# Hybrid decoder layer on one core: projection and sampled stage in one block, forget-attention queries projected last

## The reference, cut to what matters

```
z = h @ w_in                                  # 1056 tokens, 1024 -> 2848 columns
q_n, k_c, v_c, k_s, v_s, k_w, v_w, g, q_f, k_f, v_f, f = split(z)
logf = log_sigmoid(f + b_forget)
kc, vc = compress(k_c, cmp_pe[0], cmp_w1[0], cmp_w2[0]), compress(v_c, ...)   # gelu(flat @ w1) @ w2
o_n, o_f = attend_block(...)                  # compressed, selected, window branches; forgetting attention
x = x + rms_norm(concat(rms_norm(o_n), rms_norm(o_f)) @ w_o)
y = x + rms_norm((silu(hf @ w_gate) * (hf @ w_up)) @ w_down)
```

## Time and profile before

| | us |
|---|---|
| median of 3 runs | 1807.78 (1803.63 to 1809.15) |
| the profiled execution, its own time | 1804.37 |
| its span, first to last instruction | 1802.7 |
| PE busy | 1719.0, 95% of the span |
| DVE / ACT / POOL busy | 1008.4 / 724.4 / 304.3 |
| projection's last product ends, us from the start of the span | 315.5 |
| first matmul with w1 | 338.69 |

### The profile page before, as it was taken

One profiled execution on the slowest core, in us unless ns is written; L12 is line 12 of the kernel. 1 busy time (PEld: TensorE's weight loads), 2 busy tenths in 40 slices (PEclk: granted clock), 3 DMA queues, 4 the chain that ended last, 5 costly groups with the idle time before them and its releaser, 6 DMA issues.

```text
span 1802.7 us, 35393 instructions
## 1 busy us (share of the span) xinstructions
PE 1719.0 (95%) x13557; PEld 1573.7 (87%) x13557; DVE 1008.4 (56%) x1892; ACT 724.4 (40%) x1439; POOL 304.3 (17%) x629
## 2 busy tenths in 40 slices
PE   8999999799887999999999999999999999999998
PEld 6999999676665888788876899999999999999998
DVE  4533342223364666666665577766566664566565
ACT  5101010222233777777875541333333332344343
POOL 3000015320503435354430000000000000000000
PEclk9999999899998999999999999999999999999998
DMA  5547976645999212030202242232222325131112
GB/s 140 193 132 185 228 221 117 191 144 175 310 341 285 77 28 81 14 94 1 95 1 77 83 144 67 73 104 75 72 72 76 103 72 222 60 123 48 44 47 103
DMA packets 146081, 212.63 MB, mean 118 GB/s; under 512 B 23993, under 2 KB 102248, under 8 KB 145858
## 3 DMA queue, kind: packets, MB, share of 16 engines
q1 hardware_dynamic: 114114, 143.36, 24.9%
q0 software_dynamic: 16480, 52.41, 9.5%
q10 hardware_dynamic: 15328, 14.72, 3.4%
HBM read 163.11 MB, written 51.49 MB: 119 GB/s over the span
## 4 chain that ended last, share of the span: by engine, by line
PE 69%; DVE 6%; ACT 3%; issue 2%; DMA 1%; POOL 0%; DVEq 0%; SPq 0%; ACTq 0%
PE psum L195 14%; PE psum L197 13%; PE psum L196 13%; PE psum L2112 5%; PE psum L2085 5%; PE psum L1177 4%; PE psum L2076 3%; PE psum L2077 2%; PE psum L1198 2%; DMA fox_ring<-in_cache_fox_kv 1%; PE psum L1240 1%; PE psum L2120 1%; PE psum L1159 1%; PE psum L2105 1%; ACT h_parts L3182 1%
## 5 line engine op out<-in xcount | busy, mean ns | idle before, releaser
L195 PE MATMUL psum<-h_parts,down_hi 128*128 128x352 f32 x528 | 171.7, 325 | 5.9 <-DVE h_parts L3383 4.3
L195 PE MATMUL psum<-x_hi,w_hi 128*128 128x352 f32 x528 | 170.7, 323 | 1.3 <-issue 1.3
L196 PE MATMUL psum<-h_parts,down_hi 128*128 128x352 f32 x528 | 170.5, 323 | 0.0
L197 PE MATMUL psum<-h_parts,down_lo 128*128 128x352 f32 x528 | 170.5, 323 | 0.0
L196 PE MATMUL psum<-x_lo,w_hi 128*128 128x352 f32 x528 | 170.4, 323 | 0.0
L197 PE MATMUL psum<-x_hi,w_lo 128*128 128x352 f32 x528 | 170.3, 323 | 0.0
L195 PE MATMUL psum<-hf_hi,op_hi 128*128 128x264 f32 x576 | 163.5, 284 | 0.6 <-DVE silu L3364 0.6
L197 PE MATMUL psum<-hf_hi,op_lo 128*128 128x264 f32 x576 | 163.5, 284 | 0.0
L196 PE MATMUL psum<-hf_lo,op_hi 128*128 128x264 f32 x576 | 163.3, 284 | 0.0
L2165 ACT ACTIVATE probs<-psum,neg_max 128x640 f32<-128x640 f32 (+7 forms) x192 | 139.8, 728 | 18.3 <-DVE neg_max L2323 9.0
L2085 PE MATMUL psum<-ident,probs 128*128 128x128 f32 x848 | 129.1, 277 | 4.0 <-ACT probs L2165 2.4
(11 more groups left out here) (455 smaller groups left out, 4254.3 us busy)
## 6 DMA issues: line engine op xcount, KB each, us to landing
fox_ring<-in_cache_fox_kv SPq DMA_DIRECT2D x128, 256.0 KB, 6.1
zT<-z_stage SPq DMA_DIRECT2D x22, 528.0 KB, 4.4
w_ring<-in_w_in POOLq DMA_DIRECT2D x22, 512.0 KB, 5.5
down_ring<-in_w_ffn_down SPq DMA_DIRECT2D x44, 256.0 KB, 2.7
raw<-in_w_ffn_gate SPq DMA_DIRECT2D x9, 1024.0 KB, 7.8
raw<-in_w_ffn_up SPq DMA_DIRECT2D x9, 1024.0 KB, 5.4
h_dram<-stage POOLq DMA_DIRECT2D x8, 1056.0 KB, 6.0
nsa_page<-in_cache_nsa_kv POOLq DMA_DIRECT2D x64, 128.0 KB, 6.2
```

What stands on the lines that cost most here:

```text
L195: nc.tensor.matmul(dst, w_hi, x_hi, start=start, stop=False, skip_group_check=onto)
L196: nc.tensor.matmul(dst, w_hi, x_lo, start=False, stop=False, skip_group_check=onto)
L197: return nc.tensor.matmul(dst, w_lo, x_hi, start=False, stop=stop, skip_group_check=onto)
```

## The change

The two blocks become one: `build_a` and `build_b` write into the same block, no barrier stands between them. A function `projected(eng)` waits until all stores of `zT` and `nat` have landed; SP waits for it at the end of the projection as before, and now POOL, ACT and DVE wait for it too ahead of their first work of the sampled stage (POOL also for the last `take` and the key parts). PE has no such wait: its first job in each bank waits for `z_copied` of the last tile in that bank (and for the turns' copies in banks 6 and 7). The plan's order becomes q_n, nsa_kv, win_kv, fox_kv, q_f. `w1` is issued in the q_n group; the pages of sequences 0 to 3 are issued one sequence after each pair of fox_kv; the last 16 forget rows go four at a time after each pair of fox_kv, not in a seam. `load_sampled` waits for the tiles ahead of q_f, loads the fox slices of `k_new`, and no longer loads `q_fox`, whose 8 loads now stand on POOL's queue behind `load_nsa(0)`. POOL reads its 32 page numbers ahead of the waits.

```diff
-             dict(name="win_kv", col=1024, pairs=1, turn=True), dict(name="q_f", col=1304, pairs=2, turn=False),
-             dict(name="fox_kv", col=1816, pairs=4, turn=True)]
+             dict(name="win_kv", col=1024, pairs=1, turn=True), dict(name="fox_kv", col=1816, pairs=4, turn=True),
+             dict(name="q_f", col=1304, pairs=2, turn=False)]
...
-        build_a(nc, a, o, c, env)
         middle = root.enter_context(ExitStack())
         env["block"] = middle.enter_context(nc.Block())
...
+        build_a(nc, a, o, c, env)
         build_b(nc, a, o, c, env)
...
+def projected(eng, env):
+
+    for s in range(2):
+        eng.wait_ge(env["zt_stored"][s], 16 + 16 * (NZ // 2))
+        eng.wait_ge(env["nat_stored"][s], NAT_STORED[s])
...
-        block = ctx.enter_context(nc.Block())
+        block = env["block"]
...
-                loop(sp, l["pairs"], pair)
+                if l["name"] == "fox_kv":
+                    for i in range(l["pairs"]):
+                        pair(i)
+                        load_lf(1, range(PAGES // 2 + i * PAGES // 8, PAGES // 2 + (i + 1) * PAGES // 8))
+                else:
+                    loop(sp, l["pairs"], pair)
...
-                        pool.dma_start(q_fox[e * DH:(e + 1) * DH, :, p * 40 + e * TS:p * 40 + (e + 1) * TS],
-                                       zT[TILE["q_f"] + p, e * DH:(e + 1) * DH, T:N].rearrange("d (s t) -> d s t", t=TS)).then_inc(new_loaded, 16)
+                    pool.dma_start(k_new[:, 2:6, :], zT[TILE["fox_kv"]:TILE["fox_kv"] + 4, :, T:N].rearrange("n p t -> p n t")).then_inc(new_loaded, 16)
...
-                if l["name"] == "q_f":
-                    act.wait_ge(gf_stored, 64)
+                if l["name"] == "q_n":
...
+                if l["name"] == "fox_kv":
+                    act.wait_ge(gf_stored, 64)
                     act.wait_ge(pages_loaded, 16)
-                    for b in range(4):
-                        load_sequence(act, a, pages, chunks, b, chunk_loaded[b // 2])
...
                     pair(i, [s for s in range(2) if l["n0"] + 2 * i + s in KEY_TILES])
+                    if l["name"] == "fox_kv":
+                        load_sequence(act, a, pages, chunks, i, chunk_loaded[i // 2])
...
-            pool.memset(chunksT[:, :, :, 4, :], 0.0).then_inc(cleared, 1)
-            pool.dma_start(k_new[:, 2:6, :], zT[TILE["fox_kv"]:TILE["fox_kv"] + 4, :, T:N].rearrange("n p t -> p n t")).then_inc(new_loaded, 16)
             pool.wait_ge(pages_loaded, 16)
             read_four(0)
+            pool.wait_ge(z_copied, NZ + 2)
+            projected(pool, env)
+            pool.wait_ge(env["key_stored"], 64 * len(KEY_TILES))
+            pool.memset(chunksT[:, :, :, 4, :], 0.0).then_inc(cleared, 1)
             load_nsa(0)
+            with nc.allow_non_contiguous_dma(reason="four tokens of a head"):
+                for h in range(H):
+                    p, e = h // 2, h % 2
+                    pool.dma_start(q_fox[e * DH:(e + 1) * DH, :, p * 40 + e * TS:p * 40 + (e + 1) * TS],
...
+                else:
+                    pe.wait_ge(z_copied, NZ + 1 if B.bank[job] < 3 else NZ + 2)
+                    if B.bank[job] >= 6:
+                        pe.wait_ge(turn_copied, 2 + 3 * NTURN)
...
+            projected(act, env)
             for st in range(2):
...
+            projected(dve, env)
             for st in range(2):
```

More of the change, by code:

```diff
@@ L171, in program @@
         env = dict(locals())
-        build_a(nc, a, o, c, env)
         middle = root.enter_context(ExitStack())
         env["block"] = middle.enter_context(nc.Block())
+        env["z_copied"], env["turn_copied"], env["key_stored"] = sem("z_copied"), sem("turn_copied"), sem("key_stored")
+        env["zt_stored"], env["nat_stored"] = [sem(f"zt_stored{s}") for s in range(2)], [sem(f"nat_stored{s}") for s in range(2)]
+        build_a(nc, a, o, c, env)
         build_b(nc, a, o, c, env)
@@ L289, in build_a @@
         key_high, key_low = env["key_high"], env["key_low"]
-        key_high_set, key_low_set, key_stored = sem("key_high_set"), sem("key_low_set"), sem("key_stored")
+        key_high_set, key_low_set, key_stored = sem("key_high_set"), sem("key_low_set"), env["key_stored"]
         key_parts = env["key_parts"]
@@ L306, in build_a @@
         z_done = sem("z_done")
-        z_copied = sem("z_copied")
-        zt_stored = [sem(f"zt_stored{s}") for s in range(2)]
+        z_copied, turn_copied, zt_stored, nat_stored = (env[k] for k in ("z_copied", "turn_copied", "zt_stored", "nat_stored"))
         turned = sem("turned")
-        turn_copied = sem("turn_copied")
-        nat_stored = [sem(f"nat_stored{s}") for s in range(2)]
         gf_stored = sem("gf_stored")
@@ L315, in build_a, with load_lf @@
         W = a["w_in"][0].rearrange("(k p) n -> p k n", p=P)
-        block = ctx.enter_context(nc.Block())
+        block = env["block"]
         @block.sync
         def _(sp):
-            def load_lf(r, half):
-                for p in range(half * PAGES // 2, (half + 1) * PAGES // 2):
+            def load_lf(r, rows):
+                for p in rows:
                     for q in range(SEQ4):
@@ L372, in _ @@
                     sp.wait_ge(pages_loaded, 16)
[L373 to L377, removed]
+                if l["name"] in LF_SEAM:
+                    r, half = LF_SEAM[l["name"]]
+                    load_lf(r, range(half * PAGES // 2, (half + 1) * PAGES // 2))
+            projected(sp, env)
             sp.wait_ge(gf_stored, 64)
@@ L766, in _ @@
                         pair(i, ahead=n + 2 < NZ, keys=[s for s in range(2) if n + s in KEY_TILES])
-LF_SEAM = {"q_n": (0, 0), "nsa_kv": (0, 1), "win_kv": (1, 0), "q_f": (1, 1)}
+LF_SEAM = {"q_n": (0, 0), "nsa_kv": (0, 1), "win_kv": (1, 0)}
 def loop(eng, count, body):
@@ L942, in build_b @@
     zT, oT_dram, kc_dram, vc_dram = (env[k] for k in ("zT", "oT_dram", "kc_dram", "vc_dram"))
+    z_copied, turn_copied = env["z_copied"], env["turn_copied"]
     lf_loaded, w2_loaded, cleared, setup_loaded, new_loaded = (env[k] for k in ("lf_loaded", "w2_loaded", "cleared", "setup_loaded", "new_loaded"))
@@ L1095, in load_nsa @@
                         pool.dma_start(nsa_page[:, p, q, :], a["cache_nsa_kv"][0, bass.ds(ids[p, q], 1)].rearrange("o p a g d -> (o p) (a g d)")[:, 2 * P:4 * P]).then_inc(nsa_loaded[p // 4], 16)
-            pool.memset(chunksT[:, :, :, 4, :], 0.0).then_inc(cleared, 1)
-            pool.dma_start(k_new[:, 2:6, :], zT[TILE["fox_kv"]:TILE["fox_kv"] + 4, :, T:N].rearrange("n p t -> p n t")).then_inc(new_loaded, 16)
             pool.wait_ge(pages_loaded, 16)
             read_four(0)
+            pool.wait_ge(z_copied, NZ + 2)
+            projected(pool, env)
+            pool.wait_ge(env["key_stored"], 64 * len(KEY_TILES))
+            pool.memset(chunksT[:, :, :, 4, :], 0.0).then_inc(cleared, 1)
             load_nsa(0)
+            with nc.allow_non_contiguous_dma(reason="four tokens of a head"):
+                for h in range(H):
+                    p, e = h // 2, h % 2
+                    pool.dma_start(q_fox[e * DH:(e + 1) * DH, :, p * 40 + e * TS:p * 40 + (e + 1) * TS],
+                                   zT[TILE["q_f"] + p, e * DH:(e + 1) * DH, T:N].rearrange("d (s t) -> d s t", t=TS)).then_inc(new_loaded, 16)
             for r in range(RN):
```

## The result

The changed kernel is slower: 1813.09 us median of 10 runs (1809.65 to 1819.05), against 1807.54 us for the kernel before (10 runs, 1803.28 to 1811.13). The ratio is 1.0032, with a 95% interval of 1.0017 to 1.0046, some 3 to 8 us. I had forecast 1803.6 and at most 1808.5. The profiled execution took 1810.57 us, with a span of 1808.9 us against 1802.7.

The account below looks back on a forecast made before the run. PE, busy 95% of the span, was taken as the bound. Turn, takes, store landing and copies put the first w1 matmul at 334.5, not 338.69: 4.2 us saved, 1800.2 profiled, 1803.6 as median; range 1797.5 to 1808.5.

Parts of the forecast that it names:

- The turn moves ahead of q_f, the last product at 319.3: End of projection: all seven fox turns come before the last product, at 3.76 us; it ends at 319.3, not 315.52.
- The last takes: End of projection: `bias_tab` lands at 319.3, tile 20's take waits to 312.3 at no cost, tile 21's runs 319.5 to 320.9.
- The new wait: ACT and DVE copy pages only after the last `z_stage` store lands, 4.8 us after its issue at 321.1: 325.9.
- The copies: Page copies before the first w1 matmul: 7.4 us, 0.7 for position rows and signal, 0.5 for low clock: 334.5.
- Edit (d): POOL's queue: `q_fox` behind `load_nsa(0)`; POOL's list up to there starts at 327.9 instead of 346.94, at no cost.
- (a): First group: loading w1 there, 19.25 us of issue on ACT's queue, costs nothing.
- (b): Fox pairs: one sequence's pages per pair, 10.9 us of ACT's queue in 26.8 us, costs nothing.
- (c): Fox pairs: four forget rows each, 4.7 us of SP's queue ahead of a store due 11.5 us later, cost nothing.
- slower, `bias_tab` reaches over the end: Rival, chance 0.06: `bias_tab` delays tile 21's take; slower from 46.6 us of landing on; at 52 us, 5.4 us slower, 1813.2.
- The wait is only moved: Rival, chance 0.12: store landing replaces the barrier wait, 6.9 us and low clock; first w1 matmul 1.4 us earlier, 1806.4.
- Everything falls well: Rival, chance 0.25: last store lands in 2.7 us, no low clock in the second 128 matmuls; 8.5 us saved, 1799.3.
- The rule on turns between queues: `z_stage` stores beside `bias_tab`: DMA engines alternate queues packet by packet, so about twice a store's time, not ten times.

Follow-up runs that it names:

- experiment 1: The changed kernel with POOL's wait for the landing of `bias_tab` moved behind its 32 page reads: 1803.63 us, ratio 0.9975 to the kernel before.
- experiment 2: The changed kernel with POOL's 32 page reads made twice: 1831.19 us, ratio 1.013 to the kernel before.
- experiment 3: The changed kernel with POOL's clearing of `chunksT` and its waits put ahead of the 32 page reads again: 1804.25 us, ratio 0.9974 to the kernel before.
- experiment 4: The changed kernel with DVE's copy of the position rows moved from its 4th page copy to behind its 8th: 1807.3 us, ratio 0.9989 to the kernel before.
- experiment 10: Experiment 1's kernel with `bias_tab` issued on ACT's queue behind the third fox pair's pages: 1801.87 us, ratio 0.9957 to the kernel before.
- experiment 8: The changed kernel with the store of `bias_tab` issued in the first group: 1812.68 us, ratio 1.003 to the kernel before.
- experiment 6: The changed kernel with two blocks and the barrier back, and POOL's clearing ahead of the page reads: 1805.8 us, ratio 0.9984 to the kernel before.
- experiment 7: The kernel before with only the loads of `w1` moved to the first group: 1806.63 us, ratio 1.0 to the kernel before.
- experiment 9: The kernel before with the store of `bias_tab` issued in the first group: 1817.26 us, ratio 1.0047 to the kernel before.

## Why the prediction was wrong

The result lies above the range, and on the other side. By its own steps:

*The turn moves ahead of q_f, the last product at 319.3*: right, 319.3, with some luck in the digits, since it ends between 317.7 and 320.0 in the kernels with nearly the same projection (experiments 1 to 4 and 10). *The last takes*: right in kind. `bias_tab` landed after 38.4 us and not 42.2, the store of tile 18 after 29.5 us and not 26.0, so tile 20's take was at 316.1 and not 312.3, and cost nothing; the last take began at 319.51 (forecast 319.5). *The new wait*: right, copies at 326.5 against 325.9.

*The copies*: wrong, and through what I had put down as free. Edit (d) reads "POOL's whole list up to there starts at 327.9 ... since page numbers are read beforehand". The step that failed is that "beforehand": I had not asked what stands ahead of the reads on POOL. It is the wait for `bias_tab`, and I had worked out myself that it would last until 319.3; with 32 reads (16.5 us of them showed ahead of the loads) that gives 335.8 for the clearing from the rows before the change, though the exact meeting with the measured 335.78 is luck (released at 315.7, reads of 19.5 us). I also had read "POOL's clearing" as standing behind the new wait alone, and had not gone through who waits for it: DVE, in the middle of its eight copies. The sum has no term for it. In the changed kernel DVE stood still for 7.27 us for it, and by experiments 1 and 3, which take this one thing away in two ways, it made the distance from the first copy to the first w1 some 4.9 us longer.

A second term was too small: the copies themselves, 7.4 + 0.7 us and 0.5 for a low clock, 8.6 together. Without the late clearing they took 10.4 and 10.5 us at a granted clock of 0.62, and 7.8 only where the clock stayed at 1.00 (experiments 8 and 10). From copies that start at 326.5 that gives 337.0, 1.7 us before 338.69 and not 4.2. So the one block would have saved less than I wrote even with the clearing in its place; that the first w1 of experiment 3 meets 334.5 and the median of experiment 1 meets 1803.6 is in good part luck, by the early start of these executions and by the part of the medians that I can't place.

*Edits at nothing*: (a), (b) and (c) were right: experiment 6 has all of them and the new order, and is no slower than before (0.9984, 0.9968 to 1.0); experiment 7 shows (a) by itself. The earlier `load_nsa(0)` gains nothing: right (experiment 3).

*The rivals*: "slower, `bias_tab` reaches over the end" named the right transfer and the wrong way. It needed a landing after 46.6 us; it landed after 38.4, and the kernel was slower through POOL's list, not through the store of tile 19. "The wait is only moved" is what the trace looks like at first (ACT idle for 53.36 us until `zT` landed), but ACT was done at 334.8 and not the last. "Everything falls well" had the early store right as a thing to be had: with `bias_tab` out of the way (experiment 10) the last store lands in 2.7 us and the first w1 is at 332.4. The low clock in a run of 128 matmuls only moved in the changed kernel: 18.89 us was the second before, 18.70 is the first now. In experiments 1, 3, 6 and 8 it did stay away, 17.20 us in both runs, as that rival has it.

*The rule on turns between queues* (the Trainium skill, DMA: Bandwidth & Descriptors, section "Queues, rings and completion order"): I had written that the trace doesn't agree unless the packets of `bias_tab` are far slower than the others. They are. In the trace of the changed kernel it is 336 packets of 4608 bytes, 0.74 us each at the median and never more than eight at once, where a packet of a `z_stage` store (4224 bytes) takes 0.16 us. The factor of two was mine and rested on packets of like duration. So these runs don't speak against the rule; they don't prove it either, nor does any show whether what the rule calls a packet is what the trace counts as one. By the Trainium skill's rule and these durations a store beside `bias_tab` would be slowed 5 to 6 times (an estimate: 0.74 + 0.16 over 0.16). The stores took 26.0 us, 29.5 us in the changed kernel and 25.6 us in experiment 9, at quite another place, where 2.7 is usual: some ten times, so even this leaves about half open. Why the packets are slow is left open: no run separates it.

## What to carry to other kernels

When a step is moved past a wait, write down the whole list of its engine around the new place: what is ahead of it, when that is released, and who waits in the middle of what for the step itself. A clearing of 1.8 us behind 20 us of register reads cost some 5 us, three times the 1.6 us of the barrier that had been taken away. Where one store slows all others, don't only move it early: find the stretch in which nobody is due to wait for a store.

## What the hardware showed that I had not expected

Reading 32 page numbers into POOL's registers is not free: 0.29 us a read at the median, with the steps around it 16.5 to 20 us for all, and in experiment 1, where they begin at 291.1 beside `bias_tab`, 37.5 us. And a store of 1.5 MB whose source is 8 partitions takes 38 to 43 us to land at either end of the projection; beside it, `z_stage` stores go from 2.7 to as much as 29.5 us, and weight loads from 5.5 us (the page's median) to as much as 35.2.
